# Differential attention of a two-block network: rotations placed beside the products, both maps of a unit scored together from PSUM

## What is computed

```python
def rope_2d(x, tabs):      # applied to q and k of the 512 tokens, not to the context
    ...
    return jnp.concatenate([_rot(xr, cr, sr), _rot(xcol, cc, sc)], axis=-1)

def diff_attend(q, k, v, lam):
    s = jnp.einsum('bqhcd,bkhcd->bhcqk', q, k) * (q.shape[-1] ** -0.5)
    p = jax.nn.softmax(s.astype(jnp.float32), axis=-1)
    a = (p[:, :, 0] - lam * p[:, :, 1]).astype(v.dtype)
    return jnp.einsum('bhqk,bkhd->bqhd', a, v)
```

## Time and profile before

| | |
|---|---|
| median of 3 runs | 4822.42 us (4822.33 to 4823.9) |
| the profiled execution | 4819.14 us, span 4817.4 us |
| PE busy | 4411.8 us (92%) |
| DVE busy | 1426.8 us (30%) |
| ACT busy | 1002.2 us (21%) |
| POOL busy | 100.0 us (2%) |
| largest group of all, PE products L326 | 2139.3 us |
| mean granted clock of PE | 0.964 of full |

### The profile page before, as it was taken

How to read it: one execution, slowest core, us unless ns; L and a number is a source line. 1 busy time by engine, 2 the same in 40 slices (tenths; PEclk the granted TensorE clock), 3 DMA queues, 4 the chain that set the end, 5 groups by cost and what they waited for, 6 DMA issues and landing times. The chain is left out here.

```text
span 4817.4 us, 62989 instructions
## 1 busy us (share of the span) xinstructions
PE 4411.8 (92%) x28228; PEld 2722.9 (57%) x28228; DVE 1426.8 (30%) x2148; ACT 1002.2 (21%) x1817; POOL 100.0 (2%) x87
## 2 busy tenths in 40 slices
PE   7999999999999789988999689999899989969887
PEld 6888799677888545545555433333345454433333
DVE  1585744422230221336211210111214171120112
ACT  2113422201110311425111211111314051121111
POOL 0000022000000000000000000000000000000000
PEclk9999999899999999999999889999999999989999
DMA  2583200222222211010111379888211102159996
GB/s 81 201 283 112 67 4 4 77 74 79 70 76 60 61 35 59 23 35 1 53 53 53 131 295 353 312 330 319 70 47 47 53 1 87 70 207 427 427 427 256
DMA packets 187942, 652.82 MB, mean 136 GB/s; under 512 B 10934, under 2 KB 75126, under 8 KB 163110
## 3 DMA queue, kind: packets, MB, share of 16 engines
q1 hardware_dynamic: 184038, 635.09, 35.2%
q0 software_dynamic: 3648, 13.88, 0.9%
HBM read 635.71 MB, written 11.67 MB: 134 GB/s over the span
## 5 line engine op out<-in xcount | busy, mean ns | idle before, releaser
L326 PE MATMUL psum<-arena 128*128 128x264 f32 (+5 forms) x7520 | 2139.3, 446 | 56.7 <-ACT arena L996 19.2
L326 PEld LDWEIGHTS psum<-arena 128*128 128x128 f32 (+1 forms) x7520 | 1433.8, 192 | 745.7 <-issue 322.4
L908 PE MATMUL psum<-arena 128*64 128x512 f32 x3072 | 701.0, 603 | 49.2 <-DMA arena<-in_w_e 44.8
L908 PEld LDWEIGHTS psum<-arena 128*64 128x64 f32 x3072 | 213.1, 138 | 476.7 <-issue 426.6
L1902 PE MATMUL psum<-arena 64*64 64x64 f32 x7488 | 227.8, 219 | 9.6 <-issue 4.5
L651 PE MATMUL psum<-arena 128*128 128x512 f32 x544 | 234.4, 592 | 0.0
L1902 PEld LDWEIGHTS psum<-arena 64*64 64x64 f32 x7488 | 225.9, 135 | 12.3 <-issue 7.7
L1591 DVE SCALAR_TENSOR_TENSOR arena<-psum,arena 128x512 f32<-128x512 f32 (+1 forms) x160 | 110.7, 697 | 379.0 <-PE psum L888 372.1
L1575 DVE TENSOR_TENSOR arena<-arena,psum 128x512 f32<-128x512 f32 x32 | 22.0, 687 | 612.3 <-PE psum L914 330.7
L914 PE MATMUL psum<-arena 128*32 128x256 f32 x3072 | 185.7, 382 | 0.0
L651 PEld LDWEIGHTS psum<-arena 128*128 128x128 f32 x544 | 103.4, 190 | 129.5 <-issue 128.7
(11 more groups left out here) (314 smaller groups left out, 3392.5 us busy)
## 6 DMA issues: line engine op xcount, KB each, us to landing
arena<-in_w_e SPq DMA_DIRECT2D x192, 2048.0 KB, 14.4
arena<-in_w_in SPq DMA_DIRECT2D x38, 2048.0 KB, 7.9
arena<-in_w_ada SPq DMA_DIRECT2D x24, 2048.0 KB, 8.7
arena<-in_ffn_up SPq DMA_DIRECT2D x22, 1024.0 KB, 7.6
arena<-in_w_branch SPq DMA_DIRECT2D x6, 2048.0 KB, 7.7
arena<-in_ffn_down SPq DMA_DIRECT2D x8, 1408.0 KB, 7.0
arena<-in_w_in SPq DMA_DIRECT2D x16, 512.0 KB, 4.4
arena<-in_w_out SPq DMA_DIRECT2D x4, 2048.0 KB, 7.9
```

Of the source, the lines that this page charges most:

```text
L326: mm = pe.matmul(PS[0:m, 2 * region + c, 0:cn], w[0:kp, k, j * P:j * P + m], rhs(k, c0, cn), start=(k == 0), stop=(k == s.kt - 1))
L908: mm = pe.matmul(PS[c * HD:c * HD + HD, b + (m > 0), :], x(kk), w[:, k, c * BW:c * BW + BW], start=(kk == 0), stop=(kk == KT - 1))
```

## The change

1. *Rotations.* PE does the key rotations 0 to 3 behind value tiles 0 to 3, query rotations 4 to 6 behind query tiles 1 to 3, and the last behind the query products (`rotate`). Each waits for its own tile's copy only. The score of head h waits for rotation 5 + h; unit 1 also for DVE's last read of the rotation's banks. DVE's scratch for the rotation moves beside the tables.
2. *Scale.* ACT's copy of the query tiles carries the factor 1/8.
3. *Scores.* Both maps of a unit are scored together, 384 + 384 columns (256 where short), alternating between rows 0 to 63 and rows 64 to 127. A map takes a pair of banks, three pairs in turn (banks 0 to 5).
4. *Softmax from PSUM.* DVE takes the largest value from PSUM, ACT reads PSUM for the exponential and writes SBUF. The copies with scale (two of ACT, two of DVE a unit) are gone. One reciprocal serves both maps.
5. *POOL* scales map 1 (new line L1280 of the changed kernel), DVE only subtracts.
6. *Turning in two rounds* through bank 6: four tiles, ACT's copy, then two tiles and ACT's second copy. The gather has bank 7 alone, and waits until the result before is out.

```diff
         def _(pe):
+            def differences():
+                def scores(n):
+                    h, own, q = da[n]
+                    wt(pe, "rope_done", 5 + h)
+                    if n == 1:
+                        wt(pe, "rope_t", 8)
+                    if n:
+                        wt(pe, "da_e", 2 * n - 1)
+                    cn = CTX if own else T2 // 2
+                    for c in range(1 if own else 2):
+                        for m in range(2):
+                            r = slice(m * HD, m * HD + HD)
+                            mm = pe.matmul(PS[:, DA_BANK(n, m) + c, 0:cn], A[r, QR + h * T2 + q:QR + h * T2 + q + P],
+                                           A[r, KR + h * T2 + c * cn:KR + h * T2 + c * cn + cn], start=True, stop=True)
+                    inc(mm, "da_s")
+                def turn(n, part):
+                    if part == 0:
+                        wt(pe, "da_p", n + 1)
+                        if n:
+                            wt(pe, "da_c", n)
+                            wt(pe, "da_c2", n_full[n - 1])
+                    else:
+                        wt(pe, "da_c", n + 1)
...
+                for n in range(len(da) + 3):
+                    if n < len(da):
+                        scores(n)
+                    if 2 <= n < len(da) + 2:
+                        turn(n - 2, 0)
                     if n >= 3:
...
+                        gather(n - 3)
+                    if 2 <= n < len(da) + 2 and not da[n - 2][1]:
+                        turn(n - 2, 1)
...
-            by_token(f"vb{l}", range(T2 // P))
-            products(pe, f"qb{l}", rhs)
-
-            pe.wait_ge(*taken(f"qb{l}"))
-            for n in range(8):
+
+            def rotate(n):
+                name, i = ("kb", n) if n < 4 else ("qb", n - 4)
+                pe.wait_ge(*taken(f"{name}{l}", i + 1))
                 if n >= 4:
                     wt(pe, "rope_t", n - 3)
...
+            by_token(f"vb{l}", range(T2 // P), beside=lambda n: rotate(n) if n < 4 else None)
+            products(pe, f"qb{l}", rhs, beside=lambda t: rotate(3 + t) if t else None)
+            rotate(7)
+            differences()
...
         def _(act):
...
+                for n in range(len(da) + 3):
+                    if 2 <= n < len(da) + 2:
+                        take_turned(n - 2, 0)
+                    if n < len(da):
+                        power(n, 0)
+                    if 2 <= n < len(da) + 2 and not da[n - 2][1]:
+                        take_turned(n - 2, 1)
+                    if n >= 3:
+                        take_out(n - 3)
+                    if n < len(da):
+                        power(n, 1)
...
         def _(pool):
...
+            for n in range(len(da)):
+                x1 = at(DA_S(n, 1), DA_KEYS(n))
+                wt(pool, "da_r", n + 1)
+                inc(nc.gpsimd.tensor_scalar(x1, x1, at(cell(n, 2) + 1, 1), at(LAMC, 1), ALU.mult, ALU.mult), "da_x1")
...
         def _(dve):
...
+                for n in range(len(da) + 1):
+                    if n < len(da):
+                        largest(n, 0)
+                    if n:
+                        inverse(n - 1)
+                    if n < len(da):
+                        largest(n, 1)
+                    if n:
+                        normal(n - 1)
```

More of the change, by code:

```diff
@@ L464, in attention_units @@
         for h in range(DA_H):
-            for q in q_ctx + [CTX + n * P for n in range(SEQ // P)]:
-                own = q < CTX
-                maps = []
-                for p0 in (0, HD):
-                    row = lambda o, c, n: A[p0:p0 + HD, o + h * T2 + c:o + h * T2 + c + n]
-                    maps.append((row(QR, q, P), row(KR, 0, CTX), None if own else row(KR, CTX, SEQ)))
-                da.append(dict(maps=maps, nk=2 if own else 6, v=lambda t, h=h: at(VR + t * BW + h * P, P), m=P,
-                               p0=0, out=at(YB + h * T2 + q, P)))
-        return na, da
-    def counts(units):
-        jobs = [(n, kx is not None) for n, u in enumerate(units) for _, _, kx in u["maps"]]
-        seq_jobs = [sum(s for _, s in jobs[j % 2:j + 1:2]) for j in range(len(jobs))]
-        seq_units = [sum(u["nk"] > 4 for u in units[:n + 1]) for n in range(len(units))]
-        return seq_jobs, seq_units
+            da += [(h, True, q) for q in q_ctx] + [(h, False, CTX + n * P) for n in range(SEQ // P)]
+        return na, da
     def cols(w, first):
@@ L524, in layer @@
         NA_S = lambda n: H + n % 3 * 2 * BW
-        DA_S = lambda j: SCR + j % 6 * T2
+        DA_S = lambda n, m: SCR + (n % 3 * 2 + m) * T2
+        DA_KEYS = lambda n: CTX if da[n][1] else T2
+        DA_BANK = lambda n, m: (2 * n + m) % 3 * 2
+        n_full = [sum(not own for _, own, _ in da[:n + 1]) for n in range(len(da))]
         NA_P = lambda n: (H + 6 * BW, YB)[n % 2]
@@ L536, in layer @@
         SUB = SCR + KT * T2 // 2
[L537 to L538 removed]
+        ATT_SCALE = HD ** -0.5
+        assert ATT_SCALE == 2.0 ** -3
         n_norm = [ln_n["pe"]]
@@ L638, in _, with by_token @@
             rhs = lambda k, c0, cn: at(hb(k) + c0, cn)
-            def by_token(name, tiles, columns=False):
+            def by_token(name, tiles, columns=False, beside=None):
                 s = st[name]
@@ L652, in by_token @@
                     mm.then_inc(S("acc_full"), 1)
+                    if beside:
+                        beside(n)
             ln_pe(pe, xk, T2, [(S("mod_ready"), base.get("mod_ready", 0) + 1)], center=False)
@@ L1001, in _ @@
                    pre=[(S("mod_ready"), base.get("mod_ready", 0) + 1)])
-            q_at = lambda r: (lambda i, acc, j: nc.scalar.activation(
-                spread(at(r + q0 + i * T2, nq), nqc), acc, ACT.Copy))
             def near_rows(r, scale, own):
@@ L1037, in _ @@
             take(act, f"va{l}", v_at)
-            take(act, f"qa{l}", near_rows(QR, NA_SCALE, not last))
+            take(act, f"qa{l}", near_rows(QR, ATT_SCALE, not last))
             def neighbours():
@@ L1121, in _ @@
             neighbours()
+            wt(act, "lam_dot", 1)
+            inc(nc.scalar.activation(at(LAMS, 2), at(LAMS, 2), ACT.Exp), "lam_exp")
             take(act, f"kb{l}", k_at(KR))
             take(act, f"vb{l}", v_at)
-            take(act, f"qb{l}", q_at(QR))
-            wt(act, "lam_dot", 1)
-            inc(nc.scalar.activation(at(LAMS, 2), at(LAMS, 2), ACT.Exp), "lam_exp")
-            attend(da, "da", DA_S, DA_P, DA_SCALE, 6)
+            take(act, f"qb{l}", lambda i, acc, j: nc.scalar.activation(
+                spread(at(QR + q0 + i * T2, nq), nqc), acc, ACT.Copy, scale=ATT_SCALE))
@@ new lines, in differences, with largest, inverse, normal @@
+            def differences():
+                def largest(n, m):
+                    wt(dve, "da_s", n + 1)
+                    b = DA_BANK(n, m)
+                    src = PS[:, b, 0:CTX] if da[n][1] else PS[:, b:b + 2, 0:T2 // 2]
+                    inc(V.tensor_reduce(at(cell(n, 0) + m, 1), src, AX.X if da[n][1] else AX.XY, ALU.max, negate=True), "da_max")
+                def inverse(n):
+                    wt(dve, "da_e", 2 * n + 2)
+                    inc(V.reciprocal(at(cell(n, 2), 2), at(cell(n, 1), 2)), "da_r")
+                def normal(n):
+                    x, x1 = (at(DA_S(n, m), DA_KEYS(n)) for m in range(2))
+                    wt(dve, "da_x1", n + 1)
+                    inc(V.scalar_tensor_tensor(out=x, in0=x, scalar=at(cell(n, 2), 1), in1=x1, op0=ALU.mult,
+                                               op1=ALU.subtract), "da_p")
+                for n in range(len(da) + 1):
[5 more added lines that the diff above has]
+                        largest(n, 1)
+                    if n:
+                        normal(n - 1)
```

163 lines of the change are left out of this document (37 added, 126 removed).

## The result

The changed kernel takes **4759.08 us** (median of 4 runs, 4756.01 to 4760.28), the kernel before beside it 4823.16 (4822.33 to 4824.62): a ratio of 0.9865, 95% interval 0.985 to 0.9881, 64 us faster. Forecast was 4754 (4734 to 4780). The profiled execution took 4760.28 us, span 4758.3 (before 4819.14 and 4817.4).

The account below looks back on a forecast made before the run. DVE was taken to bound the attention (5.40 us a full unit) and the gaps before it. Rotations 16.6 plus attention 51.8, 68.4 us, off 4819.1 gave 4750.7; the median 3.3 above: 4754 us, range 4734 to 4780.

Parts of the forecast that it names:

- The likeliest case: Whole kernel: the time comes out as worked out, 4754 us; chance 0.60.
- Rotations: Before the attention: six inside the product stream, +5.4 us a layer, then 1.8 us to scoring; with DVE's lateness, gain 16.6.
- The period: Attention, full units: a loop through three queues sets 3.8 us a unit (3.5 to 4.3); the attention gains 51.8 us.
- The way through turn and copy: Attention, full unit: scores 1.48, transposes 0.53, drain 0.17, ACT's copy 0.49, exponential 0.92, three handovers of 0.07: 3.8 us.
- The start of the attention: First scores wait while DVE rotates two tiles serially: 2.5 us (layer 0) and 1.6 us (layer 1) go back.
- Attention without the start: Layer 1's attention: 15 x 3.8 us and some 12 us for the last unit's chain, 69.0 us against 94.9.
- POOL, T = 1.3: Attention: POOL's scale of map 1 takes T = 1.3 us a full unit; POOL's loop decides from T = 1.6.
- Both rivals on POOL: Attention: POOL sets the pace, loop 2.2 + T; T = 1.9 gives 4763 us (chance 0.14), T = 5 4863 (0.03).
- the slower side: Attention: POOL's pass so slow that the gain is gone from T = 3.7; 4863 us at T = 5; chance 0.03.
- Pairs: Attention scores: rival that the two maps' products do not overlap, period 5.1 us, +41 us, 4795; chance 0.08.
- POOL and DVE disturb each other: Attention: DVE's largest value stretched by 1.06 us beside POOL, DVE's sum 4.0, +6 us, 4760; chance 0.09.
- rotations don't hide: Product stream before the attention: PE, in order, waits for ACT's copy at each rotation, +10 us, 4764; chance 0.06.

Follow-up runs that it names:

- copy_on_dve: The `values_last` kernel with the copy of the four turned tiles moved from ACT to DVE and map 0's score products first: 4748.98 us.
- gather_half: The changed kernel with three of the six value products of a full unit in the gather (two where short): 4753.49 us.
- values_last: The changed kernel with query products ahead of value products, so DVE finishes all rotations before the attention: 4748.74 us.
- filled_wait: The changed kernel with four spare PE products into idle bank 6, three before unit 1's scores, one before unit 2's: 4749.72 us.

## Why the prediction was right, and where it was off

The likeliest case came: 4759.1 for 4754, in the range, by the mechanism named.

- **Rotations.** Six stand in the stream without idle (0.86 us each for the 0.90 taken), the first score comes 1.9 to 2.1 us behind the last product for 1.8. Right. Before DVE's lateness I had 20.7 us, the trace gives 31.1 - 10.3 = 20.8.
- **The period.** 3.8 forecast, 3.81 measured, in each kernel that left the loop alone, with POOL's pass or without, with half the gather or all of it. Two things inside it were off and cancelled, which is luck, if a small one: I had no read of the sum (0.99 for the 0.92 of the exponential), and too much for handovers (0.14 for 0.21). The way through turn and copy that I named is the one that ends last. I left out the one through DVE's largest value; it is only some 0.1 us shorter, so taking the copy out brings no more than 0.12 (`copy_on_dve`). That PE's sum is not the bound, in spite of 97%, `gather_half` shows; I had it at 3.5, and it is 3.64.
- **The start of the attention** (DVE's lateness) is the step that failed. I had 2.5 and 1.6 us of waiting there, 4.1, and nothing behind it. The wait itself is there and was sized fairly (layer 1: 3.57 us of PE idle ahead of the second score, 2.17 in `values_last`; layer 0: 3.25 and 1.22). But the clock falls behind PE's waits, and the next units pay for it: 5.8 us by `filled_wait`. In layer 1 this hangs on the lateness, for `values_last` keeps the clock up there. In layer 0 it mostly does not: `values_last` still loses 2.1 us in its first two full units, behind waits of 1.55 us and less. The attention gained 43.8 us for the forecast 47.7 (51.8 less 4.1), and all stages 64.6 for 68.4; the 5.8 us are more than what is missing, so other terms were a little too careful. I had put the low clock only into the high end of the period, for the steady state, where it did not come.
- **Attention without the start:** 69.0 forecast for layer 1, 69.40 in `values_last`. Short units 2.9 us for 2.8 (six units 2147.26 to 2168.27 are 21.0 us, four full ones 15.2).
- **POOL, T = 1.3:** measured 0.98, below the 1.6 from which it decides. Both rivals on POOL had the right loop, 2.1 + T for my 2.2 + T: at T = 2.06 the period is 4.16, at T = 5.3 it is 7.41, and the kernel is slower than before. For the slower side the price was too low, 109 us at T = 5 for a measured 128.6 at 5.3, since T counts 1.08 a pass and the tail and the short units were left out.
- **Pairs.** They overlap. Had they not, the kernel would have been no faster than before (4828.6), not 4795: the forecast of that rival lacked the low clock too.
- **POOL and DVE disturb each other, rotations don't hide:** neither came; largest value 0.94 beside POOL, no idle at the rotations.

The signs that I named for the profile hold (scores 3.81 apart, PE above 90% at full clock, DVE idle on POOL 0.37 us a unit) but for the length of the attention: 95.33 and 73.99 for 93.7 and 70.6 with the lateness.

## What to carry to other kernels

When a change makes PE the tight engine, look at the waits where the stage begins: a wait of PE costs its own length and can cost the lower clock for the units that follow. Moving the late work ahead of something long (here: queries before values) takes the wait away by a small edit; whether the clock stays up has to be read from the trace, layer by layer (here it did in one of two). Find the pace as a loop through the queues, and take every chain that reaches the same instruction; an engine at 97% may still not be the bound, and an offload (here POOL's) brings little while its old queue has room.

## What the runs showed of the chip

- After 3.57 us of idle, PE's scores ran at 1.2 GHz (2.93 us for 1.56) for two units with waits of 2.17 and less between them. In layer 1 of `values_last`, with two waits of 2.17 us behind dense products, they stayed at 2.4; in its layer 0, with short scores of 0.70 us between waits of 1.22, 1.21 and 1.55 us, they fell to 1.2 all the same. So no length of a single wait tells the two apart. With spare products in the waits they stayed at 2.4 in both layers. The Trainium skill (TensorE: Matmul & The Clock Gate, the HAM clock gate) says that the clock goes to its lower level when the array idles; the traces agree.
- The 64-row products of both maps take 1.49 or 1.50 us to the next instruction in either order, and 2.74 on the same rows.
- POOL's scale by two per-partition scalars took 982 ns for 768 elements and 0.56 us for 256, 0.83 ns for each element more; DVE's took 671 ns for 768. I had taken 1.3 us from POOL's two-input pass.
